# Twelve norm statistics of the mixer and four of the linear heads, summed from high and low parts in a two-layer hybrid trunk

## The reference, cut to what matters

```python
def rms_norm(x, gain):
    y = xf * lax.rsqrt(jnp.mean(xf * xf, axis=-1, keepdims=True) + RMS_EPS)
    return (y * gain).astype(x.dtype)

h = rms_norm(x, attn_norm[l])
(g_q, g_k, g_v, g_gate, g_lr, d_q, d_k, d_v, i_q, i_k, i_w, m_cq, m_ckv, m_kr) = split_columns(h @ w_in)
o_gla = rms_norm(gla(...), gla_out_norm) * silu(g_gate)     # per head of 128
q_d, k_d = rms_norm(d_q, dsa_q_norm), rms_norm(d_k, dsa_k_norm)   # per head of 64
q_m = rms_norm(rms_norm(m_cq) @ w_uq, mla_q_norm)           # latent of 192, heads of 96
k_m = rms_norm(concat(k_nope, k_rope), mla_k_norm)          # from rms_norm(m_ckv), 128
x = x + concat(o_gla, rms_norm(o_dsa), rms_norm(o_mla)) @ w_out
x = x + square(relu(rms_norm(x) @ w_up)) @ w_down
```

## Time and profile before

| | |
|---|---|
| median of 3 runs | 1255.1 us (1255.06 to 1255.46) |
| the profiled execution | 1255.26 us, its span 1253.5 us |
| PE busy | 1237.1 us (99%) |
| DVE busy | 751.8 us (60%) |
| ACT busy | 528.8 us (42%) |
| POOL busy | 217.1 us (17%) |
| chain that ended last | PE 92%, ACT 3%, DVE 3%, issue 1%, DMA 1% |
| granted clock of TensorE | 1.00 |

### The profile page before, as it was taken

How to read it: one execution, slowest core, us unless ns; L and a number is a source line. 1 busy time by engine, 2 the same in 40 slices (tenths; PEclk the granted TensorE clock), 3 DMA queues, 4 the chain that set the end, 5 groups by cost and what they waited for, 6 DMA issues and landing times.

```text
span 1253.5 us, 17688 instructions
## 1 busy us (share of the span) xinstructions
PE 1237.1 (99%) x5956; PEld 973.9 (78%) x5956; DVE 751.8 (60%) x1233; ACT 528.8 (42%) x858; POOL 217.1 (17%) x141
## 2 busy tenths in 40 slices
PE   9999999999999999999999999999999999999998
PEld 7766876688888888888886668767888888888887
DVE  6689868644644554544756898685446445445444
ACT  5674438644223224224436643586432242232331
POOL 1122330020120110200621334200201102102002
PEclk9999999999999999999999999999999999999999
DMA  6212220033233223323222212201232223233223
GB/s 245 86 51 67 68 85 2 18 101 123 92 101 100 98 86 100 100 88 99 98 85 85 67 51 85 68 2 40 95 100 87 99 100 101 84 100 100 96 94 111
DMA packets 30720, 108.36 MB, mean 86 GB/s; under 512 B 3536, under 2 KB 3536, under 8 KB 30672
## 3 DMA queue, kind: packets, MB, share of 16 engines
q1 hardware_dynamic: 29520, 103.82, 24.9%
q0 software_dynamic: 432, 2.86, 0.6%
q10 hardware_dynamic: 720, 1.07, 0.3%
HBM read 105.64 MB, written 2.10 MB: 86 GB/s over the span
## 4 chain that ended last, share of the span: by engine, by line
PE 92%; ACT 3%; DVE 3%; issue 1%; DMA 1%; ACTq 0%; DVEq 0%
PE bank L889 19%; PE bank L890 19%; PE bank L891 19%; PE bank L510 6%; PE bank L512 6%; PE bank L511 6%; PE bank L533 2%; PE bank L532 2%; PE bank L531 2%; PE bank L546 2%; PE bank L772 2%; PE bank L784 1%; PE bank L799 1%; PE bank L750 1%; DMA x<-in_x 1%
## 5 line engine op out<-in xcount | busy, mean ns | idle before, releaser
L944 ACT ACTIVATE wh<-raw 128x1024 fp32r<-128x1024 f32 x191 | 201.6, 1055 | 382.7 <-PE bank L891 246.5
L1267 DVE TENSOR_TENSOR wl<-raw,wh 128x1024 fp32r<-128x1024 f32 x155 | 241.2, 1556 | 75.8 <-ACT wh L944 75.7
L889 PE MATMUL bank<-hh,wl 128*128 128x512 f32 x512 | 200.0, 391 | 0.0
L889 PE MATMUL bank<-xmh,wl 128*128 128x512 f32 x512 | 199.3, 389 | 0.0
L891 PE MATMUL bank<-hl,wh 128*128 128x512 f32 x512 | 199.2, 389 | 0.0
L890 PE MATMUL bank<-xmh,wh 128*128 128x512 f32 x512 | 199.2, 389 | 0.0
L891 PE MATMUL bank<-xml,wh 128*128 128x512 f32 x512 | 199.2, 389 | 0.0
L890 PE MATMUL bank<-hh,wh 128*128 128x512 f32 x512 | 199.2, 389 | 0.0
L476 POOL TENSOR_TENSOR x<-x,rsb 128x512 f32<-128x512 f32 x63 | 83.3, 1322 | 589.3 <-DVE rsb L1688 589.3
L510 PE MATMUL bank<-xgh,wl 128*128 128x512 f32 x368 | 151.3, 411 | 3.6 <-DVE xgl L1280 3.4
L1677 DVE TENSOR_TENSOR sqb<-tf 128x512 f32<-128x512 f32 x64 | 44.3, 692 | 181.6 <-ACT hh L1230 181.6
(11 more groups left out here) (215 smaller groups left out, 1641.5 us busy)
## 6 DMA issues: line engine op xcount, KB each, us to landing
raw<-in_stream SPq DMA_DIRECT2D x191, 512.0 KB, 3.3
out_y<-x SPq DMA_DIRECT2D x8, 256.0 KB, 3.6
x<-in_x ACTq DMA_DIRECT2D x4, 256.0 KB, 6.9
x<-in_x SPq DMA_DIRECT2D x4, 256.0 KB, 7.2
con<-in_consts POOLq DMA_DIRECT2D x1, 976.5 KB, 5.2
par<-in_params POOLq DMA_DIRECT2D x1, 916.0 KB, 5.0
par<-in_params POOLq DMA_DIRECT2D x1, 896.0 KB, 6.9
raw<-in_stream SPq DMA_DIRECT2D x2, 256.0 KB, 4.2
```

The lines of the kernel that those rows point to most:

```text
L889: pe.matmul(B.t[s][:], wl[:, s, n_block(k)], src_h[:, k], start=(k == 0), stop=False)
L944: act.activation(wh[:, s], raw[:, s], ACT.Copy).then_inc(hi_ready.sem, 1)
L1267: vec.tensor_tensor(wl[:, s], raw[:, s], wh[:, s], ALU.subtract).then_inc(lo_ready.sem, 1)
```

## The change

Sixteen of the 21 statistics are summed from two fp32r parts. ACT squares into `sqb` as before, waits for that, and copies the square to an fp32r tile (high); DVE subtracts it from the square (low, fp32r); PE multiplies fp32r ones by high and by low into the same bank, two fp32r matmuls in the place of one fp32 matmul. Four of the sixteen are the `gst` statistics in the attention, whose low parts DVE makes in the turn before PE uses them. The parts lie in tiles that are free at the time (`sqh`, `sql`, `mixh`, `mixl`). Beside that:

- The ones and the block matrix exist in fp32r as well (`ones_r`, `blk_r`).
- The relevance scores get a fourth tile (`RELS`), in the place of `gg`.
- The square of `ckv` goes ahead of `relevant(3)`, and that of `dq0` ahead of the factor of `ckv`.
- The selection makes 3 steps in place of 4 in slots 9 and 10, 2 for 3 in slot 14, and 5, 5 and 4 for 4, 4 and 3 in slots 19 to 21.
- At the end of layer 0, DVE makes the low part of chunk 6 ahead of the last share, and adds the last share to x itself, in POOL's place.

```diff
-ACT_LINKS = 2
+RELS = 4
+N_PARTS = 16
+ACT_LINKS = 2 + N_PARTS
...
+        def square_of(name):
+            i = norm_index(name)
+            return (sqh[:, i % 2], sql[:, i % 2]) if i < N_PARTS - GLA_H else (mixh[:, i % 2], mixl[:, i % 2])
+        def relu_of(i, n):
+            return rel[:, i % RELS, 0:n] if i % RELS < RELS - 1 else rel_last[:, 0:n]
...
-                for d in range(KB - final):
+                for d in range(KB - 1):
                     add_share(GROUPS - 1, d)
                     if d >= 1 and not final:
                         sum_square(l + 1, 0, d - 1)
                 if not final:
-                    sum_square(l + 1, 0, KB - 1)
+                    for d in (KB - 2, KB - 1):
+                        sum_square(l + 1, 0, d)
...
+            def stat_parts(l, name, lhsT, rows=P):
+                i = norm_index(name)
+                pe.wait_ge(*nsl_ready.at(l, i))
+                pe.wait_ge(*B.vacant(l, name))
+                high, low = square_of(name)
+                pe.matmul(B[name][0:rows, :], lhsT, high[0:rows], start=True, stop=False)
+                return pe.matmul(B[name][0:rows, :], lhsT, low[0:rows], start=False, stop=True)
...
-                    stat(l, f"mqst{h}", ones[0:QK, 0:QK], sq_of(f"mqst{h}")[0:QK], QK)
+                    stat_parts(l, f"mqst{h}", ones_r[0:QK, 0:QK], QK).then_inc(*B.on_fill(f"mqst{h}"))
...
-                    pe.matmul(B[name][:], blk, sq_of(name), start=True, stop=False)
-                    pe.matmul(B[name][:], turn_rows[:], cqn[:, 1], start=False, stop=True)\
+                    pe.matmul(B[name][:], turn_rows[:], cqn[:, 1], start=True, stop=False)
+                    pe.matmul(B[name][:], blk_r[:], sqh[:, i % 2], start=False, stop=False)
+                    pe.matmul(B[name][:], blk_r[:], sql[:, i % 2], start=False, stop=True)\
...
-                pe.matmul(B["cqst"][:], ones[:], sqb[:, 0], start=True, stop=False)
-                pe.matmul(B["cqst"][:], low_rows[:], lnb[:], start=False, stop=True)\
+                pe.matmul(B["cqst"][:], low_rows[:], lnb[:], start=True, stop=False)
+                pe.matmul(B["cqst"][:], ones_r[:], sqh[:, 0], start=False, stop=False)
+                pe.matmul(B["cqst"][:], ones_r[:], sql[:, 0], start=False, stop=True)\
                     .then_inc(*B.on_fill("cqst"))
-                stat(l, "ckvst", ones[:], sq_of("ckvst"))
+                stat_parts(l, "ckvst", ones_r[:]).then_inc(*B.on_fill("ckvst"))
...
-                        stat(l, f"gst{h}", ones[:], sq_of(f"gst{h}"))
+                        stat_parts(l, f"gst{h}", ones_r[:]).then_inc(*B.on_fill(f"gst{h}"))
...
             act.wait_ge(const_loaded, 16)
+            act.activation(blk_r[:], blk, ACT.Copy).then_inc(blk_ready.sem, 1)
...
+                def square_high(name, src, rows=slice(0, P), wait=None):
+                    i = norm_index(name)
+                    if wait is not None:
+                        act.wait_ge(*wait)
+                    link(act.activation(sqb[rows, i % 2], src, ACT.Square))
+                    act.activation(square_of(name)[0][rows], sqb[rows, i % 2], ACT.Copy).then_inc(nsq_ready.sem, 1)
...
-                        if i >= 3:
-                            act.wait_ge(*rel_used.at(l, i - 3))
+                        if i >= RELS:
+                            act.wait_ge(*rel_used.at(l, i - RELS))
...
-                        square("cqst", cqn[:, 0])
+                        square_high("cqst", cqn[:, 0])
                     if u == 7:
+                        square_high("ckvst", ckvn[:], wait=B.freed(l, "ckv"))
                         relevant(3)
-                        square("ckvst", ckvn[:], wait=B.freed(l, "ckv"))
...
                         factor("cqst", Q_RANK)
+                        square_high("dqst0", dqr[:, 0], wait=B.freed(l, "dq0"))
                         factor("ckvst", KV_RANK)
-                        square("dqst0", dqr[:, 0], wait=B.freed(l, "dq0"))
                         relevant(5)
...
-                        square(f"gst{i}", B[f"go{i}"][:], wait=B.filled(l, f"go{i}"))
+                        square_high(f"gst{i}", B[f"go{i}"][:], wait=B.filled(l, f"go{i}"))
...
+                def square_low(name, rows=slice(0, P)):
+                    i = norm_index(name)
+                    vec.wait_ge(*nsq_ready.at(l, i))
+                    high, low = square_of(name)
+                    vec.tensor_tensor(low[rows], sqb[rows, i % 2], high[rows], ALU.subtract)\
+                        .then_inc(nsl_ready.sem, 1)
...
                     if u == 6:
                         weighted(1)
                         weighted(2)
+                        square_low("cqst")
                     if u == 7:
+                        square_low("ckvst")
                         weighted(3)
...
+                        square_low("dqst0")
                         f = use_factor("ckvst")
...
                     if u == 9:
                         mla_turn(0)
+                        square_low("mqst0", slice(0, QK))
                         dsa_queries(0)
+                        square_low("dqst1")
                     if u == 10:
                         mla_queries(0)
                         mla_turn(1)
+                        square_low("mqst1", slice(0, QK))
                         dsa_queries(1)
+                        square_low("dkst0")
                     if u == 11:
                         mla_queries(1)
                         mla_turn(2)
+                        square_low("mqst2", slice(0, QK))
                         dsa_keys(0)
+                        square_low("dkst1")
                     if u == 12:
                         mla_queries(2)
                         mla_turn(3)
+                        square_low("mqst3", slice(0, QK))
                         dsa_keys(1)
...
                         after(vec.tensor_tensor(kT[64:QK, 3], kT[64:QK, 3], kT[64:QK, 0], ALU.add),
                               *krb_ready.at(l, 0))
+                        square_low("mkst0")
...
+                        if pr == 0:
+                            square_low("mkst1")
                         mla_keys(pr)
...
-                per_slot = {9: 4, 10: 4, 11: 3, 12: 3, 13: 3, 14: 3, 15: 3, 16: 4, 17: 4, 18: 4,
-                            19: 4, 20: 4, 21: 3, 22: 2}
+                per_slot = {9: 3, 10: 3, 11: 3, 12: 3, 13: 3, 14: 2, 15: 3, 16: 4, 17: 4, 18: 4,
+                            19: 5, 20: 5, 21: 4, 22: 2}
...
                         mask_max(j + LEAD)
+                    if j + 1 in STAT_SLOT:
+                        square_low(f"gst{STAT_SLOT[j + 1]}")
                     if j < 2:
                         states(1, j)
...
-                    for d in range(KB):
+                    for d in range(KB - 1):
                         share(GROUPS - 1, d // 2, d % 2)
                         if d >= 1:
                             gained_low(l + 1, 0, d - 1, xgh, xgl, G_ATTN)
+                    gained_low(l + 1, 0, KB - 2, xgh, xgl, G_ATTN)
+                    share(GROUPS - 1, 3, 1, lows=False)
+                    vec.wait_ge(*dn_freed[1].at(l, GROUPS * 4 - 1))
+                    vec.wait_ge(*x_ready.at(l + 1, -2))
+                    vec.tensor_tensor(x[:, KB - 1], x[:, KB - 1], rsb[:, 1], ALU.add).then_inc(x_ready.sem, 1)
+                    low_part(1, hi_ready.at(l + 1, 1))
                     gained_low(l + 1, 0, KB - 1, xgh, xgl, G_ATTN)
```

More of the change, by code:

```diff
@@ L243, in build_trunk @@
         dkn, _ = place("dkn", [P, 2, T])
-        vm, _ = place("vm", [P, TB, H * DH])
-        gated, _ = place("gated", [P, 2, T])
+        vm, vm0 = place("vm", [P, TB, H * DH])
+        gated, gated0 = place("gated", [P, 2, T])
+        sqh, _ = place("sqh", [P, 2, T], F32R, at=gated0)
+        sql, _ = place("sql", [P, 2, T], F32R, at=vm0)
+        mixh, _ = place("mixh", [P, 2, T], F32R, at=ke0)
+        mixl, _ = place("mixl", [P, 2, T], F32R, at=ke0 + 4096)
         xmh, _ = place("xmh", [P, KB, T], F32R, at=m0)
@@ L253, in build_trunk @@
         sct, _ = place("sct", [P, 2, TB, P], at=a0 + 8192)
-        gg, _ = place("gg", [P, GLA_H, T])
+        gg, gg0 = place("gg", [P, GLA_H, T])
+        rel_last, _ = place("rel_last", [P, T], at=gg0)
         sel, _ = place("sel", [P, SEL_AT[4]])
@@ L272, in build_trunk @@
         ones, _ = place("ones", [P, P])
+        ones_r, _ = place("ones_r", [P, P], F32R)
+        blk_r, _ = place("blk_r", [P, P], F32R)
         low_rows, _ = place("low_rows", [P, P])
@@ L342, in build_trunk @@
         nsq_ready = S("nsq_ready", N_NORM)
+        nsl_ready = S("nsl_ready", N_PARTS)
+        blk_ready = S("blk_ready", 0)
         nrs_ready = S("nrs_ready", N_NORM, start=1)
@@ L680, in _ @@
                 mla_q_stat(0)
-                stat(l, "dqst1", blk, sq_of("dqst1"))
+                stat_parts(l, "dqst1", blk_r[:]).then_inc(*B.on_fill("dqst1"))
                 mla_q(1)
@@ L684, in _ @@
                 mla_q_stat(1)
```

(23 more changed lines are left out.)

11 lines of the change are left out of this document (6 added, 5 removed).

## The result

The changed kernel took 1285.1 us (median of 4 runs, 1281.0 to 1288.3) where the kernel before took 1255.1 beside it: a ratio of 1.0232, with a 95% interval of 1.0208 to 1.0255. It is 30.0 us slower. The forecast was 1275.7, the range 1258 to 1284: the direction was right, the loss half again as large as its sum. The profiled execution is the fastest of the four, 1280.97 us with a span of 1279.2, so 25.7 us over that of before.

The account below looks back on a forecast made before the run. The prediction took PE's queue, busy 99% of the span, as the bound. To 1255.3 us it added 2 x 7.3 (input stages) + 2 x 3.8 (attention) - 1.8 (boundary) = 20.4, giving 1275.7 us, range 1258 to 1284.

Parts of the forecast that it names:

- PE's saving is not paid out: Input slots 9 to 13: added subtracts make them DVE-bound, so by this alone they end level with before, within 1 us.
- The port meetings: Input stage: DVE ops on two SBUF inputs wait for POOL's `wl` subtraction; 7.3 us lost a layer.
- the whole chain at `mkst0`: Slots 12 to 14: `kinv`, then the `krb` add, meet POOL at the port; PE stalls 4.8 us before `mkst0`.
- The meeting of the `weighted` op in slot 8: Slot 7/8: the second `weighted(4)` op waits 2.2 us for POOL; slot 9 starts at 77.7, before 77.45.
- The one in slot 9: Subtract for `dqst1` held behind POOL until 87.25; the end of unit 13 comes 2.1 us late.
- The input stage's 7.3 us a layer: Input projection: port meetings cost 2.1 + 5.6, less 0.4 saved at `mkst1`, a layer; bounds 5.8 and 9.0.
- The attention's 3.8 us a layer: Attention: low parts of the four gst statistics hold up DVE's queue and PE; 3.8 us lost a layer, bounds 3.0 and 4.5.
- The boundary's 1.8 us: End of layer 0: reordered last chunks of x shorten PE's wait, 1.8 us saved once, bounds 1.0 to 2.1.
- No port meetings: Rival: input slots cost 0, only attention and boundary count; 1261 us (1256 to 1267), chance 0.15.
- Paid out in full: Rival: DVE and ACT never late, all PE savings come off; 1236.6 us; chance 0.08, in full or good part.
- PE's clock falls: Rival: after the input-stage stall PE runs at its lower clock, 2.7 us more a layer; 1281 us, chance 0.12.
- what I looked for in the profile: Signs: subtract as releaser, statistics 0.23 us apart, `kinv` and `krb` above 2 us, relevance waits gone, chunk-7 wait under 0.5.

Follow-up runs that it names:

- after_port_free: The changed kernel with POOL's low-part subtraction replaced by a memset, leaving that low part out of the result: 1264.8 us, ratio 1.0076.
- no_gst_split_late: The changed kernel with fp32 gst statistics, POOL's subtraction in four pieces and five top-k steps moved to later units: 1245.6 us, ratio 0.9923.
- ring_split: The kernel before with only the fourth relevance tile, and POOL's subtraction in four pieces: 1250.9 us, ratio 0.9966.
- filler: The changed kernel with 20 discarded matmuls ahead of PE's wait for the low part of `mkst0`: 1287.1 us, ratio 1.0257.
- gst_only: The kernel before with only the four gst statistics of the attention in parts: 1267.6 us, ratio 1.0097.
- no_gst_split: The changed kernel with the four gst statistics back in fp32 and POOL's subtraction in four pieces: 1253.9 us, ratio 0.9988.
- gst_only_order: The kernel before with the four gst statistics in parts, and DVE's masked scores ahead of the first low part: 1260.9 us, ratio 1.0042.

## Why the prediction was wrong in size

**PE's saving is not paid out.** Right. after_port_free shows the step by itself: without meetings the input stages end 1.3 and 1.4 us ahead of the kernel before, of the 6.8 us a layer that statistics and relevance ring save on PE (12 x 0.40 + 2.0), and PE is 2.7 us ahead at the end of unit 13, all of it the ring's, and 0.9 ahead behind `mla_k(1)` (forecast: level within 1). With 1.35 us less for DVE in a slot and short pieces for POOL (no_gst_split_late) the stages end 3.4 and 3.7 us ahead; the ring alone, with short pieces, gives 2.4 and 2.5 of that (ring_split).

**The port meetings.** The mechanism is right, and the whole chain at `mkst0` came as worked out: with E, the end of unit 13, at 111.6, `kinv` ended at E+4.2 (forecast E+4.25), the `krb` add at E+13.1 (E+13.2), the subtract at E+13.8 (E+14.0), PE's stall was 4.9 us (4.8). The meeting of the `weighted` op in slot 8 came as well. The one in slot 9 did not: POOL asked at 85.76 and not near 84.3, the subtract beside it kept its 0.68 us, and POOL's 2.93 us show that POOL was the one that waited:

```profile
85.78 0.68 DVE L1398 TENSOR_TENSOR sql<-sqb,sqh 128x512 fp32r<-128x512 f32 x1
```

So E was 1.1 us late and not 2.1. By the traces POOL was late because the clock had fallen behind `dqst0`; in filler, where it didn't fall, POOL asked at 84.25 and the meeting of slot 9 came. In turn one came that I hadn't foreseen, a slot before the first:

```profile
67.69 3.04 DVE L1442 SCALAR_TENSOR_TENSOR sel<-rel,iws,sel 128x256 f32<-128x256 f32 x2
```

The first of these two `weighted` operations took 2.52 us, and PE waited 2.0 us at `dqst0`; where nothing meets there, in after_port_free, that wait is 0.6. So 1.5 of the 2.0 us a layer of the relevance ring went here. ring_split, 11.7 us faster than the same kernel with the long instruction, gets them: 4.3 us in two layers.

**The input stage's 7.3 us a layer** were 8.7 and 8.7. The term that failed is one that the sum had at nothing: PE's clock. It stood as a rival of its own at 2.7 us a layer, and behind the stall it costs 2.6 to 2.7 by the filler. I had treated as alternatives two things of which one brings the other: the stall that I forecast is what makes the clock fall. With the rival's 2.7 in the sum, less the 1.0 us that E was early, the stage comes to 9.0.

**The attention's 3.8 us a layer** were 4.2 and 6.1 in the profiled run, and 12.1 in all when the part stands alone. The step was right where the clock held: in gst_only gst0 ends at 192.55 (192.5 forecast), and layer 0 of the changed kernel, at clock 1.00, loses 4.2. What failed is again the clock, which the stall of 2.7 us brings down in gst_only and in layer 1 of the changed kernel:

```profile
830.00:840.00 10.00, 7.69 (x45) 5.94 (x46) 9.23 (x26) 8.26 (x20) 0.00 (x0) 0.83 0.00 0
```

**The boundary's 1.8 us** were 2.2 in the trace and 2.2 by itself.

**The sum.** 25.7 in the profiled run against 20.4: input stages +2.8, attention +2.7, the boundary 0.4 the other way. What is over is the clock's: 2.6 or so in each input stage, 2 in the attention of layer 1, less 1.0 a layer for the meeting that didn't come. The median lies 4.1 us above the profiled run, the fastest of four. The range had no term for that spread, and its upper end missed the median by 1.1 us. Why the launches differ by up to 7.3 us stays open beyond what the two traces show of slot 9.

**The rivals.** "No port meetings" asked 1261; the run without them took 1264.8, with the attention's clock (0.91 from 186 to 225) in it, and it isn't what happened. "Paid out in full" asked for a DVE of at most 8.1 us a slot. The three figures set against it, 8.63, 7.28 and 9.03, are the lengths of the slots (DVE was busy 8.30, 7.13 and 8.60 in them), and the middle one is under 8.1; with the subtracts added and a step taken out of slot 10 DVE comes to about 8.3, 8.5 and 9.3, so the conclusion holds all the same. The relieved version, 8.4 us faster than no_gst_split, points the same way, but even there most of the statistics' 9.6 us is not paid out. "PE's clock falls" asked for 1281 (1279 to 1286), and the measured time lies in there: it is what happened, but on top of the forecast's stall and not in its place. Of what I looked for in the profile most was there: the subtract as releaser (at `mkst0` the row says "issue"), statistics 0.23 us apart, `kinv` and `krb` over 2 us, and no wait of PE at the start of layer 1. The relevance waits did not go: 1.1 us stayed at their old place and 4.0 stood at `dqst0`.

## What to carry to other kernels

Where two engines share a port, the distance in time between their instructions is a resource: a change that makes one engine earlier, even by removing a wait, can start meetings that cost more than it brings. So cut the long instruction into short ones before anything around it is retimed. When a forecast contains a stall of some microseconds on TensorE, put the slower matmuls behind it into the same sum. And put nothing that waits for another engine ahead of ready work in VectorE's queue.

## What the runs showed of the hardware

- A fourth relevance tile, which only removes waits, cost 7.2 us; with POOL's instruction in four pieces the same tile gained 4.3.
- Behind a stall of 4.9 us PE ran at its lower level for 5.8 us (clock 0.52), and behind one of 3.8 us for 4.0 us or more (0.51). Behind 2.7 us it depended: 1.00 in layer 0 of the changed kernel, 0.83 in layer 1. So it did behind the 2 us at `dqst0`: 0.57 over the four us from 76 on in the changed kernel, 1.00 in filler. Behind the 1.2 us at `mkst0` in after_port_free and the 1.16 us at gst0 in gst_only_order it stayed at 1.00.
- The fall behind `dqst0` left PE's unit ending 1.5 us later than in filler and so moved POOL's next request out of a meeting, in layer 1 as in layer 0: a lower clock in one stretch decided which engines met in the next.
- POOL's subtraction in four pieces took 3.40 us where it met DVE and the whole one 2.50; DVE's operation lost 0.5 us instead of 2.2. The Trainium skill (SBUF — State Buffer, section "SBUF: two separate sides") has the port held for the whole instruction by the one that starts first. The split runs agree: what the other engine loses follows the length of the instruction.
